# Layer 0's input product in two parts instead of four, double modulation products, and copies moved to ScalarE

## What is computed

```python
mod = silu(c) @ w_mod + b_mod                    # 2048 -> 3 x 2048, one row
shift, scale, gate = split(mod, 3)
h = rms_norm(x, g_pre) * (1 + scale) + shift
proj = h @ w_in                                  # 2048 -> 5648
a_q, a_k, a_v, s_u, s_v, c_q, c_k, c_v, c_g, z = split(proj)
y_a = sliding_window_attention(rope(a_q), rope(a_k), a_v, sinks)   # 16 heads of 64
y_b = spatial_gating(gelu(s_u), gelu(s_v), ...)
y_c = rms_norm(gated_linear_attention(c_q, c_k, c_v, log_alpha))   # 4 heads of 128
out = (concat(y_a, y_b, y_c) * silu(z)) @ w_out
x = x + gate * rms_norm(out, g_post)
```

## Time and profile before

| | |
|---|---|
| profiled execution | 2864.37 us, span 2862.5 us |
| TensorE busy in the span | 2800.3 us (98%), 14486 matmuls |
| VectorE busy | 2164.9 us (76%) |
| ScalarE busy | 1518.1 us (53%) |
| GpSimd busy | 41.5 us (1%) |
| DMA | 610.87 MB, mean 213 GB/s |

### The profile page before, as it was taken

One profiled execution on the slowest core, in us unless ns is written; L12 is line 12 of the kernel. 1 busy time (PEld: TensorE's weight loads), 2 busy tenths in 40 slices (PEclk: granted clock), 3 DMA queues, 4 the chain that ended last, 5 costly groups with the idle time before them and its releaser, 6 DMA issues.

```text
span 2862.5 us, 37337 instructions
## 1 busy us (share of the span) xinstructions
PE 2800.3 (98%) x14486; PEld 2413.4 (84%) x14486; DVE 2164.9 (76%) x2815; ACT 1518.1 (53%) x2108; POOL 41.5 (1%) x49
## 2 busy tenths in 40 slices
PE   7999999999999999999999999999999999999998
PEld 5887777998889988888888888899888888888887
DVE  8999998689755576667886678755666668866788
ACT  5455544655557464644554455565546445544554
POOL 0000000000000000000000000000000000000000
PEclk9999999999999999999999999999999999999999
DMA  9997697767656454555665556664545556655564
GB/s 394 377 363 252 198 384 303 246 221 255 231 160 184 145 172 149 176 191 191 201 204 184 191 198 200 192 194 150 172 151 171 191 194 203 204 183 189 197 217 158
DMA packets 173746, 610.87 MB, mean 213 GB/s; under 512 B 19666, under 2 KB 19938, under 8 KB 173058
## 3 DMA queue, kind: packets, MB, share of 16 engines
q1 hardware_dynamic: 170770, 599.38, 61.6%
q0 software_dynamic: 1824, 6.61, 0.8%
q10 hardware_dynamic: 976, 2.51, 0.3%
HBM read 606.30 MB, written 2.11 MB: 213 GB/s over the span
## 4 chain that ended last, share of the span: by engine, by line
PE 86%; DVE 10%; ACT 2%; issue 2%; DMA 1%; SPq 0%; POOL 0%; DVEq 0%; POOLq 0%; ACTq 0%
PE ps L2333 16%; PE ps L2264 16%; PE ps L2267 16%; PE ps L2271 16%; PE ps L2343 8%; DVE w_lo L1410 2%; PE ps L2206 2%; DVE raw L1640 2%; PE ps L2310 1%; PE ps L2312 1%; PE ps L2307 1%; PE ps L2543 1%; PE ps L2316 1%; PE ps L2321 1%; PE ps L2319 1%
## 5 line engine op out<-in xcount | busy, mean ns | idle before, releaser
L1004 ACT ACTIVATE w_hi<-raw 128x1024 fp32r<-128x1024 f32 (+3 forms) x942 | 948.9, 1020 | 990.2 <-PE ps L2271 365.1
L1410 DVE TENSOR_TENSOR w_lo<-raw,w_hi 128x1024 fp32r<-128x1024 f32 (+3 forms) x942 | 1091.9, 1177 | 485.8 <-ACT w_hi L1004 481.7
L2333 PE MATMUL ps<-hT_both,w_hi 128*128 128x512 f32 x2048 | 490.6, 392 | 1.1 <-DVE u L1566 0.9
L2264 PE MATMUL ps<-w_hi,hT_both 128*128 128x512 f32 (+3 forms) x1824 | 477.2, 383 | 10.2 <-DVE proj L1612 6.9
L2271 PE MATMUL ps<-w_hi,hT_both 128*128 128x512 f32 (+3 forms) x1824 | 459.3, 373 | 0.0
L2333 PEld LDWEIGHTS ps<-hT_both,w_hi 128*128 128x128 f32 x2048 | 376.2, 188 | 74.8 <-DVE u L1566 1.3
L2267 PE MATMUL ps<-w_lo,hT_both 128*128 128x512 f32 (+3 forms) x1640 | 413.9, 374 | 1.1 <-DVE w_lo L1410 1.1
L2271 PEld LDWEIGHTS ps<-w_hi,hT_both 128*128 128x128 f32 x1824 | 338.6, 188 | 48.5
L2264 PEld LDWEIGHTS ps<-w_hi,hT_both 128*128 128x128 f32 x1824 | 326.5, 189 | 55.7 <-DVE proj L1612 10.4
L2267 PEld LDWEIGHTS ps<-w_lo,hT_both 128*128 128x128 f32 x1640 | 304.1, 188 | 45.6 <-DVE w_lo L1410 2.6
L2343 PEld LDWEIGHTS ps<-hT_both,w_lo 128*128 128x128 f32 x2048 | 262.8, 191 | 10.2
(11 more groups left out here) (309 smaller groups left out, 2601.1 us busy)
## 6 DMA issues: line engine op xcount, KB each, us to landing
raw<-in_w_up SPq DMA_DIRECT2D x256, 512.0 KB, 3.8
raw<-in_w_down SPq DMA_DIRECT2D x256, 512.0 KB, 3.6
raw<-in_w_modT SPq DMA_DIRECT2D x162, 512.0 KB, 5.8
raw<-in_w_rest SPq DMA_DIRECT2D x80, 456.0 KB, 3.4
raw<-in_w_z SPq DMA_DIRECT2D x56, 512.0 KB, 4.3
raw<-in_w_out SPq DMA_DIRECT2D x51, 512.0 KB, 3.8
raw<-in_w_oa SPq DMA_DIRECT2D x32, 512.0 KB, 3.3
raw_more<-in_w_modT SPq DMA_DIRECT2D x30, 512.0 KB, 5.8
```

The source lines that it names most:

```text
L1004: act.activation(hi_blocks(L % SPLIT_SLOTS, c, w), blocks(raw_at(G), c, w), ACT.Copy).then_inc(S.hi_ready, 1)
L1410: dve.tensor_tensor(blocks(lo_at(G), c, w), blocks(raw_at(G), c, w), hi_blocks(s, c, w).bitcast(F32), ALU.subtract).then_inc(S.group_read, 1)
L2264: pe.matmul(o, rows(hi, c, t), wh[:, c], start=start and c == 0, stop=False)
L2333: pe.matmul(ps[:, bank(job, i, f)], wh[:, c, f * P:(f + 1) * P], hT_both[:, k0 + c].rearrange("p a n -> p (a n)"), start=k0 + c == 0, stop ...
```

## The change

- The input product of layer 0 has two jobs over eight chunks each, ina0 and inb0: eight tiles by four groups, 32 steps a job. ina0 starts with tiles 0, 1 and 7 (`opening`): their first two groups, six steps, then their other two groups, six steps; then tiles 2 to 6 in order. ScalarE copies ina0's tiles, VectorE adds inb0's.
- The modulation tiles are dealt in pairs (`pace_pairs`): 16 to ina0's steps 0 to 4, 32 to its steps 6 to 28, 18 to inb0, 24 to z0; as many as before to the later jobs. A pair whose ring slots are neighbours is taken by one `mod_pair`.
- Value products of sliding attention go to banks 6 and 7. VectorE makes the reciprocals of the sums; ScalarE copies each head with its reciprocal as scale (`sliding_out`).
- In the gated linear attention ScalarE copies the last scores (`pairs[:, 2]`) and the output `oc`, from banks 6 and 7; GpSimd clears the padding of `gq`; `pairs` isn't cleared any more, since the level 0 scores are now multiplied by the identity instead of copied under a mask.

```diff
+HALF_CHUNKS = KC // 2
-    for q in range(QUARTERS):
-        yield f"in{'abcd'[q]}0", "w_in", 0, q * QC, QC, 0, C_Z, C_Z // 8
+    for q in range(2):
+        yield f"in{'ab'[q]}0", "w_in", 0, q * HALF_CHUNKS, HALF_CHUNKS, 0, C_Z, C_Z // 8
...
+        if self.opening:
+            first = [(i, j) for half in (groups[:2], groups[2:]) for i in self.opening for j in half]
+            return first + [(i, j) for i in tiles if i not in self.opening for j in groups]
...
+        def pace_pairs(total, steps):
+
+            return [2 * n for n in pace(total // 2, steps)]
...
-        parts = [(product(f"in{'abcd'[q]}0", hT, lhs0=q * QC, evac="dve" if q else "act", pinned=True),
-                  pace(16, 13) if q < QUARTERS - 1 else pace(14, 16)) for q in range(QUARTERS)]
-        parts += [(product("z0", hT), [1, 1] + pace(20, 12) + pace(6, 17)),
-                  (product("out0", hT, evac="dve", tail=1), pace(32, 30))]
-        parts += [(product("in1", hT, swept=True), [0] + pace(22, 16)),
...
+        parts = [(product("ina0", hT, pinned=True, opening=(0, 1, 7)), pace_pairs(16, 5) + [0] + pace_pairs(32, 23)),
+                 (product("inb0", hT, lhs0=HALF_CHUNKS, evac="dve", pinned=True), pace_pairs(18, 32))]
+        parts += [(product("z0", hT), [2, 0] + pace_pairs(16, 12) + pace_pairs(6, 17)),
+                  (product("out0", hT, evac="dve", tail=1), pace_pairs(32, 30))]
+        parts += [(product("in1", hT, swept=True), [0] + pace_pairs(22, 16)),
...
-        lead("ina0", *after("ina0", 0), first=1)
+        lead("ina0", *after("ina0", 0, 4, 5), first=1)
-        for q, name in enumerate(("inb0", "inc0", "ind0")):
-            lead(name, *after(name, -2, -1), first=2 * q + 2)
+        lead("inb0", *after("inb0", -4, -3, -2, -1), first=4)
...
-            pool.wait_ge(S.group_multiplied, jobs["ind0"].L)
+            pool.wait_ge(S.group_multiplied, jobs["inb0"].L + 16)
...
+                pool.wait_ge(S.neg_max_ready, len(swa.groups) * (l + 1))
+                pool.memset(gq[GDK:P, 0], 0.0).then_inc(S.gla_padded, 1)
+                pool.memset(gq[0:GDK, 1], 0.0).then_inc(S.gla_padded, 1)
+                pool.wait_ge(S.gla_padded, 2 * (l + 1))
...
+                        for g in m.joined(s - 2) if m is swa else ():
+                            sliding_out(l, g)
...
+            def sliding_out(l, g):
+
+                t, hs = swa.groups[g]
+                act.wait_ge(S.act_bank_filled, n(S.act_bank_filled))
+                act.wait_ge(S.sliding_denominators, l * len(swa.groups) + g + 1)
+                b = 6 + (n.so_far(S.act_bank_filled) - 1) % 2
+                o = swa.out(t, hs)
+                for j in range(len(hs)):
+                    a = act.activation(o[:, j], ps[:, b, j * HD:(j + 1) * HD], ACT.Copy, scale=srec[:, g % 4, j:j + 1])
+                a.then_inc(S.act_bank_drained, 1)
...
-                for _ in range(3):
-                    yield
+                bank_copy(pairs[:, 2])
+                yield
+                for t in range(TOK):
+                    bank_copy(oc[:, t * COLS:(t + 1) * COLS])
+                oc_copied[l] = n.so_far(S.act_bank_filled)
+                yield
+                yield
...
+            def side_by_side(G):
+
+                return slots[G + 1] == slots[G] + 1 and slots[G + 1] != RAW_SLOTS
+
+            def mod_products(mods):
+
+                for first, second in zip(mods[::2], mods[1::2]):
+                    G = first[3]
+                    if second[3] == G + 1 and side_by_side(G):
+                        mod_pair(*first)
+                    else:
+                        mod_product(*first)
+                        mod_product(*second)
...
-                    for m in mods_at.get(L, ()):
-                        mod_product(*m)
+                    mod_products(mods_at.get(L, ()))
...
+                        for g in (s_ - 2, s_ - 1) if m is swa and s_ else ():
+                            denominators(l, g)
                         yield
...
-                        elif s_:
+                        elif m is not swa and s_:
                             out(m, s_ - 2)
                             out(m, s_ - 1)
...
+            def denominators(l, g):
+
+                nh, r = len(swa.groups[g][1]), g % 4
+                dve.wait_ge(S.probs_ready, sliding_probs[l] + g + 1)
+                dve.reciprocal(srec[:, r, 0:nh], ssum[:, r, 0:nh]).then_inc(S.sliding_denominators, 1)
...
-                if lev > LEVELS:
-                    b = dve_bank()
-                    drained(dve.tensor_copy(pairs[:, 2], ps[:, b]))
...
-                        drained(dve.copy_predicated(pairs[:, t].rearrange("p (h n) -> p h n", h=GH),
-                                                    repeat(levels[:, 0:P], GH),
-                                                    ps[:, b].rearrange("p (h n) -> p h n", h=GH)))
+                        drained(dve.tensor_tensor(pairs[:, t].rearrange("p (h n) -> p h n", h=GH),
+                                                  ps[:, b].rearrange("p (h n) -> p h n", h=GH), repeat(ident, GH), ALU.mult))
...
-                dve.memset(gq[GDK:P, 0], 0.0)
-                dve.memset(gq[0:GDK, 1], 0.0).then_inc(S.gla_padded, 1)
-                link(dve.memset(pairs[:, 0:2], 0.0))
...
-                    drained(dve.tensor_copy(oc[:, t * COLS:(t + 1) * COLS], ps[:, b]))
+                dve.wait_ge(S.act_bank_drained, oc_copied[l])
...
-                b = dve_bank()
+                b, filled = (act_bank(), S.act_bank_filled) if m is swa else (dve_bank(), S.dve_bank_filled)
...
+                pe.wait_ge(S.act_bank_drained, n.so_far(S.act_bank_filled))
                 for t in range(TOK):
-                    b = dve_bank()
+                    b = act_bank()
```

More of the change, by code:

```diff
@@ L106, in constants @@
     t = np.arange(P)[None, :]
-    lv = [s == t]
+    lv = []
     for n in range(1, LEVELS + 1):
@@ L316, in build @@
         c_row = A1("c_row", [P, 2, GROUP])
-        levels = A1("levels", [P, P + LEVELS * P // 2], I32)
+        levels = A1("levels", [P, LEVELS * P // 2], I32)
         sgwT = at("sgwT", [P, SGG, P], F32, A1.end)
@@ L562, in product @@
             return Job(name, io[f"w_{name}"], chunks, ncols, width, lhs, col0=col0, **how)
-        parts = [(product(f"in{'abcd'[q]}0", hT, lhs0=q * QC, evac="dve" if q else "act", pinned=True),
-                  pace(16, 13) if q < QUARTERS - 1 else pace(14, 16)) for q in range(QUARTERS)]
-        parts += [(product("z0", hT), [1, 1] + pace(20, 12) + pace(6, 17)),
-                  (product("out0", hT, evac="dve", tail=1), pace(32, 30))]
-        parts += [(product("in1", hT, swept=True), [0] + pace(22, 16)),
-                  (product("rest1", hT), pace(16, 48)),
-                  (product("z1", hT), pace(16, 32)),
+        parts = [(product("ina0", hT, pinned=True, opening=(0, 1, 7)), pace_pairs(16, 5) + [0] + pace_pairs(32, 23)),
[3 more added lines that the diff above has]
+        parts += [(product("in1", hT, swept=True), [0] + pace_pairs(22, 16)),
+                  (product("rest1", hT), pace_pairs(16, 48)),
+                  (product("z1", hT), pace_pairs(16, 32)),
                   (product("out1", hT, evac="dve", tail=TAIL), ())]
@@ L622, in each_group @@
                     yield job, i, j, job.L + q
+        sliding_probs = {}
+        oc_copied = {}
         lead_first, lead_at = {}, {}
@@ L1178, in wide @@
                 for job, i, j, L, splits in ahead(order):
-                    if prev and prev[0].kind == "ina" and j == 1:
+                    if prev and prev[0].kind == "ina" and j in (1, 2):
                         evacuate(*prev)
@@ L1240, in attention @@
                         yield
+                if m is swa:
+                    sliding_probs[l] = n.so_far(S.neg_max_ready)
                 if m.halved:
@@ L1298, in mixers1 @@
                 if l == 0:
-                    d = jobs["ind0"]
+                    d = jobs["inb0"]
                     act.wait_ge(S.dve_evacuated, d.E + 6)
@@ L1607, in evacuate @@
                     return
-                if job.kind in ("inb", "inc", "ind"):
-                    if job.kind == "inb":
-                        dve.wait_ge(S.act_evacuated, jobs["ina0"].E + i + 1)
+                if job.kind == "inb":
+                    dve.wait_ge(S.act_evacuated, jobs["ina0"].E + i + 1)
                     v, b = proj[:, :, i * job.width:(i + 1) * job.width], bank(job, i, 0)
@@ L1685, in wide @@
                         evacuate(*ended.pop(0)[0:2])
-                    if prev and prev[0].kind in ("inb", "inc", "ind") and j == 1:
+                    if prev and prev[0].kind == "inb" and j == 1:
                         evacuate(*prev)
                         prev = None
-                    for m in mods_at.get(L, ()):
-                        mod_product(*m)
+                    mod_products(mods_at.get(L, ()))
                     if L == 0:
@@ L1862, in rotation1 @@
                 else:
```

(23 more changed lines are left out.)

20 lines of the change are left out of this document (10 added, 10 removed).

## The result

The changed kernel takes 2877.83 us (median of 5 runs, 2875.88 to 2878.78), the kernel before 2865.71 beside it: ratio 1.0040, 95% interval 1.0030 to 1.0051. It is slower by 12 us. 2863.5 was forecast, with a range to 2872.5. The profiled execution took 2875.88 us (span 2873.9, 11.4 more than before).

A forecast was written before the change was run, and what follows sets the result against it. TensorE was taken to bound layer 0's first input quarter and layer 1, VectorE the other three quarters. Terms 6 - 7 - 1 + 1.1 = -0.9 us gave 2863.5 us, range 2855 to 2872.5.

The forecast's parts named there:

- z0's start: z0, after layer 0's input product, starts at 212.8 us against 206.72: 6 us later (bounds 4.5 and 10).
- z0's first 14 steps: Early z0: scores and value products no longer share banks, so 7 us come back (bounds 2 and 9.2).
- rest of z0: z0 after its first steps: VectorE loses a memset and three copies, 1 us back (0 to 2).
- last linear product and y: The gated linear part's last product for out0 stands behind one more modulation tile: 1.1 us lost.
- layer 1: The same edits lie beside a full TensorE: no change, bound 3 us of loss if ScalarE's banks are late.
- the end of ina0: ina0 ends at 132 us, from TensorE at 131.0, the queue at 131.1 and VectorE at 126.
- Start of step 6: In ina0, step 6 waits for modulation tiles from the queue and starts at 62.8 us, without a wait 51.4.
- Clock behind step 6: After TensorE's idle before ina0's step 6, 6.9 us run at the lower clock: 3.4 us lost.
- inb0: Second job of layer 0's input product: 32 steps, 77.8 us, TensorE's pace, plus about 3 us of attention's turns.
- rival (a): ScalarE's scaled copies at 0.40 us each hold TensorE, z0 gives back nothing: 2871.5 us, chance 0.19.
- The weighed rule: Skill's limit of about 358 GB/s for loads would cost 15 us more; set aside for the trace's 415 GB/s.
- rival (d): The queue falls to 374 GB/s while ina0's 40 MB load, 11 us more: 2874.5 us, chance 0.04.

The follow-up runs named there:

- e8: Changed kernel without loading the second tile of each of the 24 modulation pairs of ina0, the first tile used twice (sums incomplete): 2873.7 us, ratio 1.0029.
- e5: Changed kernel with inb0 opened by the same three tiles as ina0, six of ina0's modulation tiles moving into inb0: 2871.2 us, ratio 1.0021.
- e4: Changed kernel with the sliding heads' value products back on VectorE's banks and VectorE doing the scaling: 2879.4 us, ratio 1.0053.
- e9: e7 with ScalarE's copies of a finished pair of value groups ahead of the next pair's exponentials: 2860.1 us, ratio 0.9983.
- e11: e9 with VectorE's reciprocals of a finished pair of groups ahead of the next pair's maxima: 2854.7 us, ratio 0.9959.
- e2: Changed kernel with the modulation tiles after the input product paced one by one as before: 2871.9 us, ratio 1.0022.
- e3: Changed kernel with the gated linear part's last product, diagonal block of pairs and their copies back on VectorE and its banks: 2875.3 us, ratio 1.0034.
- e6: Changed kernel with the edits of e5, e2 and e3 together: 2864.6 us, ratio 0.9997.
- e7: Changed kernel with the edits of e1, e2 and e3 together (four parts, single pacing, last linear product on VectorE): 2860.1 us, ratio 0.9982.
- e12: e11 with every modulation product after the first 16 tiles made singly: 2856.3 us, ratio 0.9966.
- e1: Changed kernel with layer 0's input product in four parts of 4 chunks again: 2863.5 us, ratio 0.9994.

## Why the prediction was wrong, by its steps

| step | forecast | measured |
|---|---|---|
| z0's start | +6 | +11.3 |
| z0's first 14 steps | -7 | -5.1 |
| rest of z0 | -1 | +0.9 |
| last linear product and y | +1.1 | +0.75 |
| layer 1 | 0 (bound 3) | +3.6 |
| sum | -0.9 | +11.4 |

The prediction failed at two steps: the end of ina0 (5.3 us of the miss) and the terms for the rest of z0 and for layer 1 (5.5 us). Neither alone takes the forecast out of its range (2863.5 + 5.5 = 2869.0); both do, with the 1.9 us that z0's first steps gave back less.

The measured terms are differences between the lags of the changed kernel at successive places: 11.3 at z0, 6.2 at its step 14, 7.1 at its last turn, 7.8 at in1, 11.5 at the end of layer 1.

*Start of step 6: 62.8 forecast, 62.87 measured, in part by luck.* The queue's sum has the last tile at 58.2, and VectorE took it at 58.00 without a wait. But VectorE's own work gives that time by itself, and e8 starts step 6 at 62.12 with half the bytes. From 33.6 us VectorE has 6 double and 4 single products, 6 low parts and 2 splits, 6 x 2.21 + 4 x 1.14 + 6 x 1.02 + 1.3 = 25.2 us, and with some 1.5 us of gaps reaches the column sums at 60.3; from 39.4 us on it waits for no load. The prediction counted VectorE over all of ina0, not up to this deadline.

*End of ina0: 132 forecast, 137.45 measured. This is the first failed step.* TensorE's own path was right (131.0; e5 ran it in 129.7). The queue at 131.1 and VectorE at 126 were set beside it, each as if the others left it alone, with 1 us for their closeness. The queue's term took a queue that never pauses. But SyncE loads only into a slot of the ring that is free, and TensorE, standing before step 6, freed none: from 61.1 to 67.7 us SyncE issued no load. Whom SyncE waited for between 55 and 85 us (in total, times, longest), and the windows behind step 6:

```profile
SPq L926 <- PE ps L2313: 19.4, 9, 6.6
```

```profile
62.90:70.50 7.60, 7.60 (x27) 6.87 (x28) 6.45 (x7) 4.18 (x7) 0.00 (x0) 0.69 1.03 417
70.50:81.50 11.00, 11.00 (x56) 10.17 (x55) 10.61 (x11) 5.95 (x9) 0.00 (x0) 1.00 0.89 309
81.50:129.20 47.70, 45.20 (x215) 38.53 (x214) 43.19 (x43) 17.08 (x22) 0.00 (x0) 1.00 1.03 416
```

The queue moved 417 and 416 GB/s around that pause and 309 in it, which is some 2.8 us of the queue's time (11.0 x (1 - 309 / 417), an estimate). ScalarE's last wait for it ended at 129.2 us, for the group before the last; 126.8 was forecast for the last. Behind that landing stand, in ScalarE's order, a rounding, a turn's copies, an evacuation, the last rounding and the next turn's copies, where the sum had only one rounding. Timeline of ScalarE in the changed kernel:

```profile
129.21 0.96 ACT L1018 ACTIVATE w_hi<-raw_more 128x900 fp32r<-128x900 f32 x1 [2.64 <-DMA raw_more<-in_w_ina]
130.07 1.00 ACT L1091 ACTIVATE hf<-ps,mod,hcol 128x256 f32<-128x256 f32 x2
131.17 0.63 ACT L1096 ACTIVATE hT_both<-hf 128x512 fp32r<-128x512 f32 x1
131.71 0.96 ACT L1037 ACTIVATE proj<-ps 128x450 f32<-128x450 f32 x2
132.56 0.96 ACT L1018 ACTIVATE w_hi<-raw_more 128x900 fp32r<-128x900 f32 x1
133.41 1.02 ACT L1091 ACTIVATE hf<-ps,mod,hcol 128x256 f32<-128x256 f32 x2
```

TensorE's last two turns, at 131.13 and 134.48, waited for the two copies into hf, and each stands ahead of a step: the last two steps started at 131.54 and 134.89. From the landing at 129.2 to the end are 8.25 us; the sum had 4.3 behind a landing that is one group later. How the 7.7 us divide between the queue, VectorE and ScalarE's order is not settled: halving the bytes gave back at least 4.05 (e8), and no run changed ScalarE's order here.

*Clock behind step 6: 3.4 us forecast, 2.2 measured* (step 6 took 4.63 us against 2.43). Another 1.6 us went in step 0, from 37.05 to 41.09: its first four matmuls took 1.84 us, as step 6's did, where later ones take 0.98. That delayed nothing that shows, since step 6 waited for VectorE.

*inb0: right.* 80.6 us against 80.8, TensorE busy throughout.

*z0's first 14 steps: mechanism right, 5.1 us back where 7 were forecast.* The 3.12 us wait had no place any more (e4 brings 3 us back). A copy with a scale costs 1.73 / 8 = 0.22 us, under the 0.28 taken. What stayed was not the copies' price, on which rival (a) hung, but their place: behind exponentials that wait 4.9 us for VectorE (e9 to e11). The prediction named the exponentials and not what they wait for.

*Rest of z0 and layer 1: the second failed step.* Forecast were 1 us back and no change; measured are 0.9 and 3.6 us lost. The prediction priced a double product at 2.22 against 2 x 1.14 and missed that pairs put two tiles into one step, so that a low part waits for both. e2 brings back 2.9 us between z0's start and in1 and 1.6 from rest1 on, e3 1.35 (a bank of ScalarE's found full, for which the prediction had a bound of 3 us and no price). "Beside a full TensorE" was no cover: VectorE prepares groups only two steps ahead of it. The 0.7 us of in1 were not pinned down, and the identity product was not run by itself (it takes 0.69 us, the predicated copy before took 0.73).

*The weighed rule.* The Trainium skill, "DMA: Bandwidth & Descriptors", section "Where 436 GB/s comes from", limits HBM to SBUF at about 358 GB/s for one core. The queue moved 417 GB/s from 34 to 62 us and 405 over ina0, so the measurement again decides against it. The time came out beyond rival (d)'s 2874.5, but not by a queue at 374 GB/s throughout: held slots did slow it, for 11 us, and TensorE held them.

## What to carry to other kernels

When work is moved ahead of a deadline, add up every engine and the queue up to that deadline, and the in-order tail behind the last landing; stage averages hide it. Ask also what an engine that stands keeps from starting: here it held the slots, and the queue ran short behind it. Two small instructions merged into one are also a longer block ahead of whatever stands behind them: pair them only where the follower has slack. When an engine takes over another's copies, put them, and what they wait for, ahead of the work that waits longest.

## What the runs showed of the hardware

A queue at a full share does not move at one rate. Windows of 10 us in in1, from 10 us behind its start, in the kernel before:

```profile
465.70:475.70 10.00, 10.00 (x48) 8.26 (x47) 9.90 (x18) 4.72 (x6) 0.00 (x0) 1.00 1.00 351
475.70:485.70 10.00, 10.00 (x47) 8.08 (x46) 10.00 (x14) 4.62 (x6) 0.00 (x0) 1.00 1.01 409
485.70:495.70 10.00, 10.00 (x48) 8.12 (x47) 10.00 (x16) 4.62 (x6) 0.00 (x0) 1.00 1.03 416
```

in e2:

```profile
470.10:480.10 10.00, 10.00 (x48) 8.25 (x47) 9.90 (x16) 4.74 (x6) 0.00 (x0) 1.00 1.03 353
480.10:490.10 10.00, 9.31 (x44) 7.37 (x43) 9.69 (x14) 4.61 (x6) 0.00 (x0) 1.00 1.01 407
490.10:500.10 10.00, 10.00 (x47) 8.21 (x46) 9.13 (x15) 4.73 (x6) 0.00 (x0) 1.00 1.01 367
500.10:510.10 10.00, 8.60 (x40) 6.79 (x39) 9.36 (x11) 4.62 (x7) 0.00 (x0) 1.00 1.03 415
```

and in e6:

```profile
476.00:486.00 10.00, 10.00 (x48) 8.24 (x47) 10.00 (x14) 4.62 (x6) 0.00 (x0) 1.00 1.01 402
486.00:496.00 10.00, 9.82 (x46) 7.77 (x45) 10.00 (x16) 4.62 (x6) 0.00 (x0) 1.00 1.03 421
```

The first of these windows moves 351 GB/s in the kernel before too, and TensorE doesn't wait there. e2 has a second slow one, 367 GB/s at a share of 1.01, and in the next TensorE waits 1.4 us for hT_both. e7, e9 and e11 have such a second window (351 to 359 GB/s, share 0.98). e6, whose in1 is dealt like e2's, has none, and its in1 loses 0.2 us; so the dealing alone doesn't make it. e12 has none either and still waits 1.2 us. Whether it belongs to what runs ahead of in1 or to single executions stays open, and with it 1 to 3 us of in1's loss in e1, e2, e4, e7 and e9.
